# Four unread 128x512 matmuls in each of the attention steps 0 to 9

## What is computed

```
proj = h @ w_in
q, k, v, qi, ki, wi, u = split(proj)        # 8 heads of 64, one k and v for all
score = sum_h wi * relu(qi_h . ki)          # index scores, 4 heads
sel   = top 128 of the admissible keys per query
attn  = softmax(q . k[sel] / 8) . v[sel]
y = gelu(s5_ssm(u))
y = y * sigmoid(y @ glu_w + glu_b)          # the GLU, 512x512 weights
x += gate * (concat(norm(attn), norm(y)) @ w_out)
```

## Time and profile before

| | |
|---|---|
| time, median of 3 runs | 2078.43 us (2076.39 to 2078.64) |
| profiled execution | 2080.41 us, span 2078.6 us |
| TensorE matmuls busy | 2009.0 us, 97% of the span, 9410 records |
| VectorE busy | 1326.2 us, 64% |
| ScalarE busy | 690.7 us, 33% |
| mean granted TensorE clock | 0.978 of full speed |
| attention steps, layer 0 / layer 1 | start at 534.95 us / 1548.34 us |

### The profile page before, as it was taken

How to read it: one execution, slowest core, us unless ns; L and a number is a source line. 1 busy time by engine, 2 the same in 40 slices (tenths; PEclk the granted TensorE clock), 3 DMA queues, 4 the chain that set the end, 5 groups by cost and what they waited for, 6 DMA issues and landing times.

```text
span 2078.6 us, 24984 instructions
## 1 busy us (share of the span) xinstructions
PE 2009.0 (97%) x9410; PEld 1611.4 (78%) x9410; DVE 1326.2 (64%) x2143; ACT 690.7 (33%) x1061; POOL 89.9 (4%) x123
## 2 busy tenths in 40 slices
PE   7999999999899999999999999998989999999998
PEld 5878888777577788888878888886766787888886
DVE  6887876576884753643468787656779566455334
ACT  4432322332453431222342322224244443222223
POOL 0000000300100000000000000040000000000000
PEclk8999999999799999999999999999997999999999
DMA  8666743342112445433248485415420136353332
GB/s 294 198 196 214 233 120 94 97 113 72 46 31 61 138 156 162 154 93 99 82 130 258 147 257 151 122 55 138 107 66 11 41 102 194 101 192 112 101 94 79
DMA packets 398480, 265.81 MB, mean 128 GB/s; under 512 B 58032, under 2 KB 374168, under 8 KB 398360
## 3 DMA queue, kind: packets, MB, share of 16 engines
q1 hardware_dynamic: 397920, 263.83, 42.7%
q10 hardware_dynamic: 440, 0.38, 0.1%
HBM read 257.35 MB, written 6.82 MB: 127 GB/s over the span
## 4 chain that ended last, share of the span: by engine, by line
PE 65%; issue 21%; DVE 8%; ACT 3%; DMA 1%; SPq 1%; POOL 0%; DVEq 0%; POOLq 0%; ACTq 0%
PE ps L1815 19%; PE ps L1816 18%; PE ps L1817 18%; PE ps L2135 2%; PE ps L2154 1%; DVE w_lo L1071 1%; DMA stage<-in_ffn_w 1%; ACT w_hi L740 1%; DVE mod_acc L1092 1%; PE ps L2162 1%; PE ps L2145 1%; PE ps L2227 1%; DVE h_lo L1152 1%; PE ps L2232 1%; PE ps L2115 1%
## 5 line engine op out<-in xcount | busy, mean ns | idle before, releaser
L1815 PE MATMUL ps<-h_hi,w_hi 128*128 128x512 f32 x1725 | 682.4, 396 | 8.4 <-DVE w_lo L1071 5.7
L1816 PE MATMUL ps<-h_lo,w_hi 128*128 128x512 f32 x1725 | 674.3, 391 | 0.0
L1817 PE MATMUL ps<-h_hi,w_lo 128*128 128x512 f32 x1725 | 674.0, 391 | 0.0
L1071 DVE TENSOR_TENSOR w_lo<-stage,w_hi 128x1024 fp32r<-128x1024 f32 (+2 forms) x322 | 375.6, 1190 | 128.7 <-ACT w_hi L740 126.7
L1815 PEld LDWEIGHTS ps<-h_hi,w_hi 128*128 128x128 f32 x1725 | 325.1, 188 | 87.3 <-issue 13.5
L740 ACT ACTIVATE w_hi<-stage 128x1024 fp32r<-128x1024 f32 (+2 forms) x322 | 318.3, 1017 | 197.2 <-PE ps L1817 177.1
L1817 PEld LDWEIGHTS ps<-h_hi,w_lo 128*128 128x128 f32 x1725 | 325.2, 189 | 69.2
L1816 PEld LDWEIGHTS ps<-h_lo,w_hi 128*128 128x128 f32 x1725 | 325.4, 189 | 65.4 <-issue 0.5
L1815 PE MATMUL ps<-g_hi,w_hi 128*128 128x512 f32 x704 | 283.0, 402 | 9.8 <-DVE x L1212 7.8
L1817 PE MATMUL ps<-g_hi,w_lo 128*128 128x512 f32 x704 | 280.4, 398 | 0.0
L1816 PE MATMUL ps<-g_lo,w_hi 128*128 128x512 f32 x704 | 280.4, 398 | 0.0
(11 more groups left out here) (333 smaller groups left out, 1633.1 us busy)
## 6 DMA issues: line engine op xcount, KB each, us to landing
stage<-in_ffn_w SPq DMA_DIRECT2D x210, 512.0 KB, 4.6
mod_stage<-in_mod_w SPq DMA_DIRECT2D x144, 512.0 KB, 5.4
stage<-in_ffn_w SPq DMA_DIRECT2D x64, 448.0 KB, 4.0
stage<-in_w_in SPq DMA_DIRECT2D x20, 512.0 KB, 3.9
mod_first<-in_mod_w SPq DMA_DIRECT2D x16, 512.0 KB, 9.4
stage<-in_w_out SPq DMA_DIRECT2D x16, 512.0 KB, 4.1
x_in<-in_x SPq DMA_DIRECT2D x4, 512.0 KB, 5.3
stage<-in_w_in SPq DMA_DIRECT2D x8, 256.0 KB, 4.5
```

What stands on the lines that cost most here:

```text
L1071: V.tensor_tensor(w_lo[:, c % RING, 0:n], stage[:, c % RING, 0:n], w_hi[:, c % RING, 0:n].bitcast(F32), ALU.subtract).then_inc(w_split_lo. ...
L1815: mm(out, hi, rhs_hi, start=first, stop=False)
L1816: mm(out, hi, rhs_lo, start=False, stop=False)
L1817: return mm(out, lo, rhs_hi, start=False, stop=last)
```

## The change

`keep_streaming(4, m0 + 12)` is called in the steps 0 to 9 as well, behind `logits(e + 1)` (and the swap of step 3) and ahead of `turn(e)`. In two layers these are 80 more matmuls of 128x128 by 128x512 and their weight loads. They use the first GLU chunk. Nothing else changes.

```diff
@@ -115,6 +115,7 @@
 INDEX_FROM = 8
 SUM_BEHIND = 2
 KEEP_FROM = 18
+KEEP_UNTIL = 10
@@ -2265,6 +2266,8 @@
                     if e in GLU_AT:
                         glu(*GLU_AT[e])
+                    if e < KEEP_UNTIL:
+                        keep_streaming(4, m0 + 12)
                     if e >= KEEP_FROM:
                         keep_streaming(3, m0 + (15 if e < 24 else 16))
                     turn(e)
```

## The result

The changed kernel took 2088.93 us, the median of 20 runs; the kernel before 2078.87 (20 runs, 2076.0 to 2081.46). The ratio is 1.005, 95% interval 1.0035 to 1.0065: 0.5% slower, where I had forecast no change that could be told. The median hides what is most telling. The 20 times lie in three groups: five at 2075.8 to 2079.3, eight at 2085.9 to 2089.9, seven at 2096.0 to 2099.8. The profiled execution, 2098.72 us (span 2096.9), is one of the last group.

What follows compares the result with a forecast made beforehand. VectorE was taken to bound steps 0 to 9, TensorE the rest. Steps start 1.8 us late but the GLU stretch gains 2.72, so 0.9 a layer: 2078.43 - 1.8 = 2076.6 us, range 2072.8 to 2089.5.

Steps and rivals of the forecast that it cites:

- The clock still falls behind step 0: Step 0: four matmuls fill 1.0 of 4.5 us idleness, about 3.5 remain, so the clock falls; chance 9 in 10.
- A low step costs 1.45 + 1.88 = 3.33 us: Attention steps at 1.2 GHz: own TensorE work 1.45 us plus four added matmuls 1.88, against a VectorE step of 2.3.
- Step 3 is another matter: Step 3 also holds the swap product of 1.86 us; its 3.74 us of dense work was to bring the clock back.
- two examples: Bounds for the clock's return: 6 us of dense feed-forward matmuls from 394, and within 4 us after 563.87, from GLU work.
- the forecast's own case: Clock falls in step 0, returns in step 3; gain 0.2 to 2 us a layer, 2074.5 to 2078; chance 0.38.
- the late case: Rival of a clock low until the GLU steps: 2089.0 us with one layer late, 2101.4 with both; chance 0.33.
- the clock stays low until the GLU steps: Steps 1 to 9 all run low and TensorE becomes the bound: 11.5 us later in that layer; chance 0.33.
- The gain at the end, 2.72 us a layer: From the values of step 9 through the first GLU step, TensorE at full clock takes 3.32 instead of 6.04 us.
- VectorE can follow: VectorE's own waits of 1.56 us for ScalarE's squares and 0.60 for values 15 go, so it keeps up.
- The clock comes back early: Steps 1 and 2 suffice to restore the clock, or it does not fall: gain 2.4 us a layer, 2073.6; chance 0.2.
- All time at the low clock is paid for now: If TensorE paced steps 0 to 9, full speed would give back half of 27 us a layer: 2051; chance 0.03.

Runs made afterwards that it cites:

- both gaps filled and four each: Changed kernel with twenty unread matmuls in step 0 and eight more ahead of logits(6) in step 5, four in steps 1 to 9: 2074.54 us, 0.9978 to before.
- three each: Twenty unread matmuls in step 0, eight ahead of logits(6) in step 5, three instead of the changed kernel's four in steps 1 to 9: 2074.32 us, ratio 0.9981.
- twelve in step 0: Changed kernel with twelve unread matmuls in step 0, eight more ahead of logits(6) in step 5, four in steps 1 to 9: 2076.41 us, 0.9987 to before.
- the first gap alone filled: Changed kernel with twenty unread matmuls in step 0, where TensorE waits for ScalarE, and four in steps 1 to 9: 2080.39 us, 1.0019 to before.
- the fills alone: Changed kernel with twenty unread matmuls in step 0 and eight ahead of logits(6) in step 5, none in other steps: 2087.91 us, 1.0035 to before.

## Why the prediction was wrong

*The clock still falls behind step 0*: right. 3.38 us of the idle time were left (forecast 3.5), and the clock was at 0.51 from 540.

*A low step costs 1.45 + 1.88 = 3.33 us*: right, 3.26.

*"Step 3 is another matter: ... so 1.86 + 1.88 = 3.74 us of dense work ... and I let it come back there"*: **this is the step that failed.** Step 3 took 552.24 - 547.27 = 4.97 us, 4.97 - 1.45 = 3.5 of it dense, and the clock stayed low behind it and behind all that followed, up to the GLU work in layer 0 and to step 9 in layer 1 of the profiled execution. My rule was a single length of dense work between two examples, and such a length does not decide: the kernel with four in steps 0 to 3 has the same list up to step 3, and there the clock came back in step 3 of layer 1 and not in that of layer 0. One of the two examples was not of dense work alone either: the GLU step stood behind nine steps whose logits, transposes and values had been running too; that this matters is not shown. By the grouping, the forecast's own case (no layer late, 2075.8 to 2079.3 against its 2074.5 to 2078) came in five executions of 20. I had given it 0.38, and the late case, which came in the other 15, 0.33. That the groups stand for none, one and both layers late is worked out (their means are 10.3 and 9.6 us apart, about a late layer's 8.8 and 7.1 and the small gain of one in time; their mean clocks are 0.986, 0.980 and 0.975, and a step of 0.006 is 0.006 x 2090 / 0.5 = 25 us at the low level, about what a return in step 9 or later instead of step 3 adds); a trace there is of the last group alone, so how the clock came back in time in the others is not shown.

*The rival "the clock stays low until the GLU steps"*: its mechanism came true, and its sum of 11.5 us for the ten steps measured 10.9. What I left out of it is that the first GLU step then meets the clock just coming back, which returns 6.04 - 3.92 = 2.1 us. So one layer late was 8.8 us, not 11.5. Both late came to 2098.7 against my 2101.4, but 2.3 us of that lie outside the attention. One term of the sum is 0.1 us too small: step 9 is 4.01 - 0.46 + 1.01 = 4.56, not 4.46; it measured 573.93 - 569.61 = 4.32.

*The gain at the end, 2.72 us a layer*: right in size: 2.9 and 3.1 us with both gaps filled and four each, and as much with three each and with twelve in step 0, in none of which the clock fell there. It was right too that VectorE can follow.

*"The clock comes back early" (2073.6)*: not seen in the changed kernel, whose best of 20 was 2075.8. Where the fall was prevented, the medians were 2074.3 and 2074.5.

*"All time at the low clock is paid for now" (2051)*: refuted. With both attentions at 1.00 throughout, the gain was 2.9 and 3.1 us, not 13.5 each. The rule of the Trainium skill, "TensorE: Matmul & The Clock Gate", section "Terms", by which the penalty is the throttled time times one minus the clock's share, does not price this stretch, in which VectorE was busy 32.85 of 34 us.

The spread was foreseen, but not its size: 24 us, where the kernel before has 5.5.

**Still open.** What decides, in one execution of one kernel, whether the clock returns in step 3 or twenty microseconds later. Nothing in the program differs. Some kernels scatter widely (2 or 4 each, 12 in step 1, the first gap alone filled) and others do not (both gaps filled with 3 or 4, 8 each, though the last in five runs only); what triggers the return is not shown. Nor is it shown where the 2 us come from that the profiled execution lost between the layers.

## What to carry to other kernels

Unread matmuls keep TensorE's clock up; they are a poor means to bring it back, since at the low level each costs twice as much (four took 1.87 us, and 1.03 at full clock with the first gap filled), just where there is least room. So first find the gap behind which the clock falls and fill that, then add to each step no more than the pace-setter covers at full clock (here 3 or 4, not 6), and check with many runs: a kernel whose clock takes different courses shows it as groups of times, not as a shift. What the whole is worth is not the time at the low level, but the difference in the stretch where TensorE is the bound: 2.9 us here, out of 27 at the low clock.

## What was unexpected of the hardware

One program, on one core, had three separate groups of times about 10 us apart (2076 to 2079, 2086 to 2090, 2096 to 2100), with mean granted clocks of 0.985 to 0.987, 0.979 to 0.982 and 0.974 to 0.976. Within one execution of the kernel with two matmuls each, the clock went up and down again in layer 0 (1.00 in 550 to 560, 0.51 in 560 to 567) and stayed at 0.50 for 30 us in layer 1, in the same sequence of instructions. And an early return can cost time: with the fills alone, in both layers, and with four in steps 0 to 3, in layer 1, the clock came back for 3 to 7 us, fell again, and two GLU steps ran low instead of one, at +3.5 to +3.8 us a layer; the second slow one is about 2 us of it.
